# Layernorm of a convolution: which engine sums the last three tiles

## What is computed

```python
def layernorm(x, g, b):
    x32 = x.astype(jnp.float32)
    mu = jnp.mean(x32, axis=-1, keepdims=True)
    var = jnp.mean(jnp.square(x32 - mu), axis=-1, keepdims=True)
    y = (x32 - mu) * lax.rsqrt(var + LN_EPS)
    return y.astype(x.dtype) * g + b

def conformer_conv_module(h, w1, b1, dw_w, dw_b, ln_g, ln_b, w2, b2):
    u = h @ w1 + b1
    a, gt = jnp.split(u, 2, axis=-1)
    u = a * jax.nn.sigmoid(gt)
    u = causal_dwconv(u, dw_w) + dw_b
    u = jax.nn.silu(layernorm(u, ln_g, ln_b))
    return u @ w2 + b2
```

## Time and profile before

| | us |
|---|---|
| median of 3 runs | 3297.73 |
| lowest, highest | 3294.17, 3299.56 |
| the profiled execution | 3292.07 |
| its span in the profile | 3290.3 |

### The profile page before, as it was taken

How to read it: one execution, slowest core, us unless ns; L and a number is a source line. 1 busy time by engine, 2 the same in 40 slices (tenths; PEclk the granted TensorE clock), 3 DMA queues, 4 the chain that set the end, 5 groups by cost and what they waited for, 6 DMA issues and landing times. The chain is left out here.

```text
span 3290.3 us, 33491 instructions
## 1 busy us (share of the span) xinstructions
PE 3096.4 (94%) x13786; PEld 2499.5 (76%) x13786; DVE 1712.3 (52%) x1776; ACT 1011.6 (31%) x1203; POOL 399.8 (12%) x161
## 2 busy tenths in 40 slices
PE   7998869899999999989999999899999999999996
PEld 3784357788888888778888877677877788888885
DVE  5697786656556554574511076577455322223225
ACT  3454444332222122233221133476222311111111
POOL 0595550000000000000200034000110000000000
PEclk9998879899999999899999999999998999999998
DMA  6114423132223331321432343531331202112112
GB/s 207 58 33 159 148 96 113 73 109 64 90 77 116 100 100 63 109 77 64 141 113 92 108 154 128 136 74 50 126 118 56 76 26 64 49 38 62 38 45 109
DMA packets 96192, 301.24 MB, mean 92 GB/s; under 512 B 11205, under 2 KB 15045, under 8 KB 95847
## 3 DMA queue, kind: packets, MB, share of 16 engines
q1 hardware_dynamic: 96040, 299.09, 27.8%
HBM read 251.34 MB, written 47.71 MB: 91 GB/s over the span
## 5 line engine op out<-in xcount | busy, mean ns | idle before, releaser
L708 PE MATMUL ps<-mainr,wh 128*128 128x512 f32 (+1 forms) x6592 | 1782.0, 390 | 29.5 <-issue 12.7
L708 PEld LDWEIGHTS ps<-mainr,wh 128*128 128x128 f32 x6592 | 1238.6, 189 | 286.6 <-issue 31.2
L708 PE MATMUL ps<-mainr,wl 128*128 128x512 f32 (+1 forms) x3296 | 1030.7, 389 | 0.0
L708 PEld LDWEIGHTS ps<-mainr,wl 128*128 128x128 f32 x3296 | 623.1, 189 | 128.6
L1713 DVE TENSOR_TENSOR wl<-raw,wh 128x1024 fp32r<-128x1024 f32 (+2 forms) x272 | 294.1, 1083 | 457.1 <-ACT wh L1235 456.9
L1235 ACT CAST wh<-raw 128x1024 fp32r<-128x1024 f32 (+2 forms) x320 | 282.0, 886 | 746.9 <-PE ps L708 538.3
L1972 DVE TENSOR_TENSOR mainf<-mainf,ps 128x1024 f32<-128x1024 f32 x80 | 97.7, 1221 | 215.0 <-PE ps L708 215.0
L754 PE MATMUL ps<-mainr,wh 128*128 128x512 f32 x576 | 164.4, 409 | 36.0 <-issue 21.8
L2013 DVE SCALAR_TENSOR_TENSOR ps<-mainf,vec,ps 128x1024 f32<-128x1024 f32 (+1 forms) x174 | 180.9, 1102 | 2.5 <-ACT ps L1424 2.3
L2497 POOL TENSOR_TENSOR tmp<-tmp,mainf 128x1024 f32<-128x1024 f32 x8 | 27.5, 3444 | 1160.6 <-DMA mainf<-in_rope 1097.5
L1049 PE MATMUL ps<-mainr,wh 128*128 128x512 f32 x512 | 160.3, 395 | 6.3 <-POOL wl L2464 6.1
(11 more groups left out here) (236 smaller groups left out, 2896.8 us busy)
## 6 DMA issues: line engine op xcount, KB each, us to landing
raw<-in_mod_w SPq DMA_DIRECT2D x48, 512.0 KB, 4.5
raw<-in_ada_w SPq DMA_DIRECT2D x48, 512.0 KB, 3.7
raw<-in_f_up SPq DMA_DIRECT2D x44, 512.0 KB, 4.2
raw<-in_g_up SPq DMA_DIRECT2D x44, 512.0 KB, 3.5
raw<-in_w_in SPq DMA_DIRECT2D x40, 512.0 KB, 4.1
raw<-in_pw SPq DMA_DIRECT2D x24, 512.0 KB, 3.6
sc_x<-mainf SPq DMA_DIRECT2D x24, 512.0 KB, 2.6
mainf<-sc_x SPq DMA_DIRECT2D x24, 512.0 KB, 6.2
```

The lines of the kernel that those rows point to most:

```text
L708: ins = e.matmul(out, wt[:, a:b], xs[n], start=kk == 0 and t == 0, stop=kk == kt - 1 and t == 2)
```

## The change

The squares of tiles 6 and 7 move, on ScalarE, from behind the steps to the head of steps 30 and 31. VectorE's additions for tiles 6, 7 and 5, six in all, are gone. TensorE makes the columns of the first five tiles' sums (`S(0)` and `lnsum`) between the products of steps 30 and 31, left open for accumulation, and after the product of step 31 six further groups of columns, of each of the tiles 6, 7 and 5 and of their squares, accumulated in the same PSUM columns. The scratch of a late square is freed by its columns and not by VectorE's addition, and the scratch of tiles 6 and 7's squares is taken from the ring at steps 30 and 31. The statistics wait for the columns of tile 5.

```diff
--- before.py
+++ after.py
@@ -249,7 +249,9 @@
 POOL_ORDER = list(pool_turns())
 SUM_ORDER = (0, 2, 3, 1, 4, 6, 7, 5)
 
-SUM_STEPS = {24: 0, 25: 2, 26: 3, 27: 1, 28: 4}
+
+SUM_STEPS = {24: 0, 25: 2, 26: 3, 27: 1, 28: 4, 30: 6, 31: 7}
+SUM_LATE = SUM_ORDER[5:]
 
 
 def convolved(i):
@@ -554,11 +556,12 @@
         bank = self.bank
         for b in range(4):
             bank.last[b] = acc.last[b // 2]
-        tmp.put(NTMP - 1, ("lnsum",), ("cols", "lnq"))
+        tmp.put(NTMP - 1, ("lnsum",), ("cols", "lnq", 0))
         tmp.only(*range(NTMP - 1))
         for kind, s in OTHER:
             if kind == "f" and SUM_STEPS.get(s):
-                tmp.take(("lnsq", SUM_STEPS[s]), ("lnqadd", SUM_STEPS[s]))
+                i = SUM_STEPS[s]
+                tmp.take(("lnsq", i), ("cols", "lnq", i) if i in SUM_LATE else ("lnqadd", i))
             if kind != "f":
                 self.mod_weights(kind, s)
                 bank.take((kind, s), *self.mod_free(kind, s))
@@ -582,11 +585,9 @@
             acc.last[n] = bank.last[2 * n] + bank.last[2 * n + 1]
         acc.only(0, 1, 2)
         acc.take(("lnmean",), ("mean",))
-        for i in SUM_ORDER[5:]:
-            tmp.take(("lnsq", i), ("lnqadd", i))
+        tmp.take(("lnsq", SUM_ORDER[-1]), ("cols", "lnq", SUM_ORDER[-1]))
         tmp.only(*range(NTMP))
-        self.aux[0].take(("cols", "ln"), ("lnstat", 0))
-        self.aux[1].take(("cols", "lnq"), ("lnstat", 2))
+        self.aux_take(("cols", "ln"), [("lnstat", 0)], [("lnstat", 2)])
         self.aux_take(("spread", "ln"), [("lnmul", ND - 1)], [("lnmul", ND - 1)])
         for i in range(ND):
             tmp.take(("ln", i), ("lnlo", i))
@@ -965,17 +966,22 @@
             turn = None
         if kind == "f":
             filter_step(s)
+            if s == 30:
+                hold_aux("cols", "ln")
+                w.wait_ge(*k.at("csum", 4))
+                end_columns(k.S(0), 3072, m.ones[:, 0:1], 1, True, False, "ln", 0)
+                w.wait_ge(*k.at("lnqadd", SUM_ORDER[4]))
+                end_columns(k.TMP("lnsum"), 3584, m.ones[:, 0:1], 1, True, False, "lnq", 0)
         else:
             modulation(kind, s)
             turn = (kind, s)
 
 
-    hold_aux("cols", "ln", banks=(0,))
-    w.wait_ge(*k.at("csum", ND - 1))
-    end_columns(k.S(0), 3072, m.ones[:, 0:1], 1, True, True, "ln")
-    hold_aux("cols", "lnq", banks=(1,))
-    w.wait_ge(*k.at("lnqadd", SUM_ORDER[-1]))
-    end_columns(k.TMP("lnsum"), 3584, m.ones[:, 0:1], 1, True, True, "lnq")
+    for i in SUM_LATE:
+        w.wait_ge(*k.at(*convolved(i)))
+        end_columns(k.CV(i), 3072, m.ones[:, 0:1], 1, False, i == SUM_LATE[-1], "ln", i)
+        w.wait_ge(*k.at("lnsq", i))
+        end_columns(k.TMP("lnsq", i), 3584, m.ones[:, 0:1], 1, False, i == SUM_LATE[-1], "lnq", i)
     hold_acc("lnmean")
     spread("mean", k.ACC("lnmean"), k.COL("rn", 0, 8), ("lnstat", 0))
     norm_spread("ln")
@@ -1470,8 +1476,7 @@
     assert made == len(POOL_ORDER)
 
 
-    for i in SUM_ORDER[5:]:
-        convolved_square(i)
+    convolved_square(SUM_ORDER[-1])
     split_to(k.W["pw2", 0] + 3)
     w.wait_ge(*k.at("lnstat", 3))
     e.activation(k.COL("rs", 0, 8), k.COL("u", 0, 8), ACT.Sqrt, bias=m.eps[LN_EPS]).then_inc(*k.to("sqrt", "ln"))
@@ -2144,7 +2149,7 @@
             row = None
         if kind == "f":
             filter_step(s)
-            if s in SUM_STEPS:
+            if s in SUM_STEPS and SUM_STEPS[s] not in SUM_LATE:
                 convolved_sum(SUM_ORDER.index(SUM_STEPS[s]))
         else:
             modulation_weights(kind, s, HL)
@@ -2152,16 +2157,14 @@
     conv_steps(turns, 1000)
 
 
-    for n in range(5, ND):
-        convolved_sum(n)
     split_to(k.W["pw2", 0] + 3)
     mean, u = k.COL("rn", 0, 8), k.COL("u", 0, 8)
-    w.wait_ge(*k.at("cols", "ln"))
+    w.wait_ge(*k.at("cols", "ln", SUM_LATE[-1]))
     e.tensor_copy(mean, m.ps[:, 3072:3088:2]).then_inc(*k.to("lnstat", 0))
     w.wait_ge(*k.at("lnstat", 0))
     e.tensor_tensor(u, mean, mean, ALU.mult).then_inc(*k.to("lnstat", 1))
     w.wait_ge(*k.at("lnstat", 1))
-    w.wait_ge(*k.at("cols", "lnq"))
+    w.wait_ge(*k.at("cols", "lnq", SUM_LATE[-1]))
     e.tensor_tensor(u, m.ps[:, 3584:3592], u, ALU.subtract).then_inc(*k.to("lnstat", 2))
     w.wait_ge(*k.at("lnstat", 2))
     e.tensor_scalar(u, u, 0.0, None, ALU.max).then_inc(*k.to("lnstat", 3))
```

## The result

| | before | after |
|---|---|---|
| median of 12 runs, us | 3293.82 | 3302.85 |
| lowest to highest | 3287.72 to 3299.56 | 3294.84 to 3309.67 |
| profiled execution, its span | 3292.07, 3290.3 | 3300.25, 3298.4 |

What follows compares the result with a forecast made beforehand. TensorE bounds most of the kernel; here tile 5's chain over ScalarE and GpSimd was to hold its last columns. Statistics at 492.0 against 483.3, 8.7 us later: 3297.73 + 8.7 = 3306.4 us, range 3295 to 3313.

Steps and rivals of the forecast that it cites:

- early pair: TensorE, first five tiles' two column groups before step 31's product: wait for tile 7's accumulator, then take 6.96 us.
- The product: TensorE, filter step 31's product behind the first five tiles' columns: 7.66 us, ending at 474.8.
- The two groups behind it: TensorE, tile 6's two column groups after step 31's product: 1.70 + 1.93 = 3.6 us, to 478.4.
- Tile 7's two groups: TensorE, columns of tile 7 and its square while tile 5 is completed: about 6.3 us, to 484.7.
- The squares on ScalarE: Squares of tiles 6 and 7 moved to steps 30 and 31: delay the step 30 copy, VectorE losing next to nothing.
- The last pair: TensorE, columns of tile 5 and its square: 6.96 us at the low clock, from 485.05 to 492.0.
- rival 1: Columns keep TensorE's clock up, tile 5's pair running fast: 3.4 to 5.3 us late, 3303 us; chance 0.17.
- rival 4: TensorE's clock stays low over the whole stage: 12 to 15 us late, 3311 us; chance 0.12.
- bounds: Limits of the predicted delay: up to 12.1, then 14.7 us at low clock; down to 5.3, then 3.4 us.
- The shared slot: Scratch slot 0: ScalarE's step 31 copy waits for tile 6's columns, to 478.4, delaying tile 5 to 485.0.
- Rival 2: Tail behind tile 5: the change works, statistics 4.7 us early, 3293.0 us, or 3289.7 at full clock; chance 0.08.
- Rival 3: The delay is real but taken up later or balanced by other stages: 3298 us; chance 0.13.

Runs made afterwards that it cites:

- e2: Changed kernel with squares of tiles 6 and 7 taking scratch slots behind the filter scratch of steps 30 and 31; last tap to statistics 31.82 us.
- e4: Changed kernel without the four column groups of tiles 6 and 7, late squares' slots freed by the squares; last tap to statistics 28.47 us.
- e1: Changed kernel with the first five tiles' two column groups moved behind step 31's product; last tap to statistics 28.28 us, ratio 1.0018 to the kernel before.
- e3: Changed kernel without the first five tiles' two column groups, accumulator wait moved behind step 31's product; last tap to statistics 21.66 us.
- e6: Kernel before with VectorE's last six additions reordered, tiles first, then squares; last tap to statistics 21.80 us, ratio 0.9982 to the kernel before.
- e9: The same kernel as e6, run again; last tap to statistics 21.33 us, ratio 0.9997 to the kernel before.
- e7: Kernel before, first five tiles' columns behind step 31's product, VectorE keeping four additions for tiles 6, 7, 5; last tap to statistics 20.46 us, ratio 1.0001.
- e5: Changed kernel with the squares of tiles 6 and 7 back behind the steps on ScalarE; last tap to statistics 35.46 us.
- e10: The same kernel as e7, run again; last tap to statistics 20.45 us, ratio 0.9996 to the kernel before.
- e8: Kernel of e6 with 40 more matmuls behind step 31's product; last tap to statistics 21.35 us, ratio 0.9999 to the kernel before.

## Why the prediction was right, point by point

Times are from the end of tile 7's last tap (460.08 in the prediction, 463.06 after).

| step | predicted | measured |
|---|---|---|
| early pair starts at once, product starts | 7.0 | 6.90 |
| product ends | 14.7 | 13.9 |
| copy of step 31 on ScalarE | 18.3 | 18.10 |
| tile 5 complete | 24.9 | 24.65 |
| tile 5's columns start | 25.0 | 24.70 |
| statistics read | 31.9 | 31.79 |

**The early pair** held the product back as counted: its first instruction was idle for 9.69 us, released by VectorE's last tap (L2018). **The product** took 7.0 and not 7.66; the clock rose sooner. **The two groups behind it** took 4.1 (1.70 + 2.38) and not 3.6 (1.70 + 1.93). **Tile 7's two groups** took 6.8 and not 6.3. Product and first two groups together leave the copy 0.2 us early. **The squares on ScalarE** cost VectorE nothing, as said: it reads the copy of step 30 2.1 us after the tap before (462.19) and 2.0 us after it now (465.07). **GpSimd's last addition** took 2.34 and not 3.20, since VectorE's additions are gone. **The last pair** took 6.9 us at the low clock; rival 1, columns that keep the clock up, is out. So is rival 4, a clock that stays low over all of it: the product's stretch below has 0.77, and the two groups behind it 0.88. In the bounds, the product's upper one is 10.4 - 7.66 = 2.7 and not 2.6, and the 2.86 of the third group of rows 8 is its length and not a time from start to start; neither moves the forecast. Stretches of the kernel after, with the columns of rows 7:

```profile
463.10:470.00 6.90, 6.88 (x33) 6.89 (x33) 4.04 (x4) 5.25 (x6) 4.35 (x2) 0.50 0.61 212
470.00:477.00 7.00, 7.00 (x26) 5.66 (x27) 1.46 (x1) 0.00 (x0) 0.38 (x1) 0.77 0.01 4
477.00:480.90 3.90, 3.90 (x33) 3.90 (x32) 0.00 (x0) 0.00 (x0) 0.00 (x0) 0.88 0.00 0
480.90:494.60 13.70, 13.70 (x65) 13.70 (x66) 2.85 (x5) 5.94 (x6) 4.70 (x2) 0.50 0.10 38
```

In the last stretch TensorE is busy for all of 13.7 us and is granted 0.50, 1.2 GHz. By the Trainium skill (TensorE: Matmul & The Clock Gate, Part 1, What's actually happening) a sustained busy engine is released to 2.4 GHz. The trace agrees for the product of step 31, whose clock rises from 0.50 on the way (0.77 over its stretch). It does not agree for these columns, and the measurement decides.

**The shared slot** is where the reasoning was off though its number fitted. The prediction made tile 5's chain over ScalarE and GpSimd the bound, with TensorE free 0.3 us before it. The two are tied: TensorE has no idle time at 487.76 and tile 5 was complete at 487.71. e2 took 3.4 us out of that chain and D did not move; e4 took the groups away too, and TensorE then waited for the chain. So the causes stand so: the pair's place 3.5 us (e1), the pair itself 6.6 (e3), and of the 11.2 us taken off VectorE the six late groups leave 1.6 of gain (e3): 3.5 + 6.6 - 1.6 = 8.5. The prediction counted the hold of the pair rightly, but took one of two equal bounds for the only one; that its number did not suffer is luck, as they end within 0.1 us of each other. **Rival 2** was wrong for this order. Its test was tile 5 complete before 476.3, which is 16.2 after the tap. e3 meets it (14.5) and gains 1.6 in D and not 4.7, since four groups still stand ahead of tile 5's. **Rival 3**, that the delay is taken up later, is out within what the ratio tells: 7.9 us at the end for 8.5 in D. In the two profiles alone, 3.4 us seem to be taken up behind the statistics (3298.4 - 494.85 = 2803.6 for 3290.3 - 483.38 = 2806.9), but the two profiles of one kernel, e6 and e9, differ there by 3.7. Median for median the rise was 9.0 us, against 8.7 predicted; the absolute time came lower, 3302.85 for 3306.4, because the median of before over 12 runs is 3293.82 and not the 3297.73 of the first three.

## What to carry to other kernels

Before work goes to the engine that stands idle, write down its queue around the place and what each added instruction waits for: here an added pair of column groups cost 10.1 us in front of a product whose results others waited for (e3), 6.6 behind it with six more groups to follow (e1 against e3), and nothing behind it where the queue had a gap (e7). A sum over tiles is cheap as an addition (1.2 us for each tile here, 3.4 beside GpSimd's additions) and dear as another group of columns (3.4 us at the low clock, 1.7 right behind a dense product). Six late groups in place of the six additions gained 1.6 in D (e3, which leaves the first five tiles out), four additions kept on VectorE gained 2.8 (e7), and neither was shown to make the whole kernel faster. When a chain and a queue end within 0.1 us of each other, shortening one of them shows nothing; take both away in separate runs before naming the bound.

## What the runs showed of the hardware

Columns run at the low clock even in a queue without gaps: 13.7 us of solid work at 0.50 in the kernel after. Behind a dense product the first group took 1.84 us (after, e1, e2, e3, e5, e7, e10), a second without a gap 1.92 to 2.46, and a third 3.35 to 3.55 (2.86 in rows 8). In e8 40 dense matmuls made a group 1.92 long even 1.05 us after their end; the next, behind 1.79 us of idleness, took 3.58. VectorE's additions lose time to GpSimd's: 3.38 and 3.35 while GpSimd adds, 1.21 when it does not the earlier trace rows. GpSimd's own second addition went from 3.20 to 2.34 when they were gone, while its first had taken 2.35 beside one of them.
